# A transformer layer in float32 on one core: where the low parts of 16 weight tiles of the down projection are made

## The reference, cut to what matters

```python
h = rms_norm(x, ffn_norm_w[layer])
gate, up = jnp.split(h @ w_gate_up[layer], 2, axis=-1)
x = x + (jax.nn.silu(gate) * up) @ w_down[layer]      # (256 x 5632) @ (5632 x 2048)
```

## Time and profile before

| | us |
|---|---|
| median of 2 runs | 1143.29 (1143.13 to 1143.45) |
| the profiled execution | 1144.9 |
| its span, first to last instruction | 1142.8 |
| lies around the span | 2.1 |

### The profile page before, as it was taken

The page is one execution under the profiler, slowest core; times in us unless marked ns, Lnnn a source line. Parts: engine busy times, 40 slices in busy tenths (PEclk is TensorE's granted clock), DMA queues, the critical chain, the costliest instruction groups (busy, mean ns, idle before and its releaser), DMA issues.

```text
span 1142.8 us, 15659 instructions
## 1 busy us (share of the span) xinstructions
PE 1129.1 (99%) x5325; PEld 949.7 (83%) x5325; DVE 821.1 (72%) x1177; ACT 605.6 (53%) x856; POOL 11.6 (1%) x63
## 2 busy tenths in 40 slices
PE   7999999999999999999999999999999999999998
PEld 7988888888888888888888888888888888878887
DVE  5588787587876575667668567567577598887777
ACT  6566766668654465344344344344344455545553
POOL 3000000000000000000000000000000000000000
PEclk9999999999999999999999999999999999999999
DMA  8666454555644456666666666666666646655564
GB/s 263 192 191 204 141 173 133 160 159 159 219 161 161 166 170 183 200 193 193 191 195 193 193 193 191 194 192 186 200 192 187 208 153 215 220 197 182 195 201 166
DMA packets 102260, 213.23 MB, mean 187 GB/s; under 512 B 7065, under 2 KB 18114, under 8 KB 101954
## 3 DMA queue, kind: packets, MB, share of 16 engines
q1 hardware_dynamic: 101346, 209.30, 59.1%
q0 software_dynamic: 560, 3.15, 0.8%
q10 hardware_dynamic: 304, 0.14, 0.0%
HBM read 210.46 MB, written 2.10 MB: 186 GB/s over the span
## 4 chain that ended last, share of the span: by engine, by line
PE 89%; DVE 6%; ACT 2%; DMA 1%; issue 1%; ACTq 0%; DVEq 0%; SPq 0%
PE main L1487 45%; PE main L1490 22%; PE side L1713 7%; PE side L1716 3%; DVE w_lo L957 1%; PE side L1611 1%; PE main L1693 1%; PE main L1691 1%; PE main L1692 1%; PE side L1691 1%; PE side L1692 1%; PE side L1693 1%; DVE w_lo L1351 1%; PE side L1510 1%; DMA raw<-in_w_in 1%
## 5 line engine op out<-in xcount | busy, mean ns | idle before, releaser
L957 DVE TENSOR_TENSOR w_lo<-raw,w_hi 128x1024 fp32r<-128x1024 f32 (+3 forms) x316 | 374.9, 1191 | 249.4 <-ACT w_hi L660 245.9
L660 ACT CAST w_hi<-raw 128x1024 fp32r<-128x1024 f32 (+3 forms) x316 | 322.6, 1025 | 390.5 <-PE main L1487 384.3
L1487 PE MATMUL main<-w_hi,hT_hi 128*128 128x512 f32 (+2 forms) x1088 | 422.4, 389 | 2.4 <-DVE hT_lo L978 1.8
L1490 PE MATMUL main<-w_hi,hT_lo 128*128 128x512 f32 (+2 forms) x1088 | 418.0, 385 | 0.0
L1487 PE MATMUL main<-w_lo,hT_hi 128*128 128x512 f32 (+2 forms) x1088 | 285.5, 384 | 0.0
L1487 PEld LDWEIGHTS main<-w_hi,hT_hi 128*128 128x128 f32 x1088 | 204.9, 188 | 41.0 <-DVE hT_lo L978 3.0
L1490 PEld LDWEIGHTS main<-w_hi,hT_lo 128*128 128x128 f32 x1088 | 205.0, 188 | 37.8
L1487 PEld LDWEIGHTS main<-w_lo,hT_hi 128*128 128x128 f32 x1088 | 203.0, 188 | 39.0
L909 ACT CAST w_hi<-raw 128x1024 fp32r<-128x1024 f32 (+1 forms) x85 | 82.5, 972 | 49.8 <-PE side L1713 19.0
L1351 DVE TENSOR_TENSOR w_lo<-raw,w_hi 128x1024 fp32r<-128x1024 f32 (+1 forms) x85 | 93.1, 1120 | 5.4 <-ACT w_hi L909 5.0
L1713 PE MATMUL side<-w_hi,aT_hi 128*128 128x512 f32 x212 | 82.6, 390 | 0.1
(11 more groups left out here) (241 smaller groups left out, 968.4 us busy)
## 6 DMA issues: line engine op xcount, KB each, us to landing
raw<-in_w_gate_up SPq DMA_DIRECT2D x176, 512.0 KB, 4.4
raw<-in_w_down SPq DMA_DIRECT2D x88, 512.0 KB, 4.5
raw<-in_w_in SPq DMA_DIRECT2D x64, 512.0 KB, 3.9
raw<-in_w_out SPq DMA_DIRECT2D x32, 512.0 KB, 3.7
raw<-in_w_in SPq DMA_DIRECT2D x15, 384.0 KB, 4.3
raw<-in_w_ukv SPq DMA_DIRECT2D x8, 512.0 KB, 3.9
raw<-in_w_uq SPq DMA_DIRECT2D x8, 384.0 KB, 3.4
raw<-in_w_in SPq DMA_DIRECT2D x8, 320.0 KB, 3.1
```

Of the source, the lines that this page charges most:

```text
L660: copy(w_hi[:, slot, 0:n], raw[:, slot, 0:n]).then_inc(s_hi, 1)
L957: tt(w_lo[:, slot, 0:n], raw[:, slot, 0:n], w_hi[:, slot, 0:n].bitcast(F32), ALU.subtract)\
L1487: m = matmul(banks[t][:, 0:cols], hi[:, at[n], tok], rhs, start=(part == "hi" and k == k_first), stop=(part == "lo" and k == last))
L1490: matmul(banks[t][:, 0:cols], lo[:, at[n], tok], rhs, start=False, stop=False)
```

## The change

Of the two S items behind most Q items the first becomes an L, also a plain k tile: 8 in each of e = 0 and e = 1, 16 of the 56 plain items. For an L, DVE does nothing. ACT makes w_hi as before, waits for its own result, and writes minus w_hi into the w_lo slot (`nc.scalar.mul` by -1). Then GpSimd, which waits for that, issues a DMA from raw to w_lo that adds what it carries to what is there: w_lo = -w_hi + raw. PE starts the 8 high matmuls of an L as soon as w_hi is there, and waits for the landing of the adding DMA (s_addlo) before its 4 low ones. SP loads again into the raw slot of an L only after that landing. `lo_count` takes the L granules out of the counts of s_lo.

```diff
-    shapes = ["S" * 11 + "QSS" * 8 + "S", "S" * 3 + "QSSQSSSS" * 4 + "S"]
+    shapes = ["S" * 11 + "QLS" * 8 + "S", "S" * 3 + "QLSQLSSS" * 4 + "S"]
...
+ADDED = [x[4] for x in DOWN_ITEMS if x[0] == "L"]
...
+def lo_count(n):
+
+    return n + 1 - sum(g <= n for g in ADDED)
...
                     sp.wait_ge(s_hi, converted)
-                    sp.wait_ge(s_lo, converted)
+                    sp.wait_ge(s_lo, lo_count(converted - 1))
+                    if converted - 1 in ADDED:
+                        sp.wait_ge(s_addlo, 16 * (ADDED.index(converted - 1) + 1))
...
+            for kind, _, _, load, n, _ in DOWN_ITEMS:
+                if kind == "L":
+                    pool.wait_ge(s_neg, ADDED.index(n) + 1)
+                    pool.dma_start(w_lo[:, n % RING, :], raw[:, load % RING, :], accum_op=ALU.add).then_inc(s_addlo, 16)
...
                         hi(n, raw[:, load % RING, :], WIDE)
+                        if kind == "L":
+                            act.wait_ge(s_hi, n + 1)
+                            nc.scalar.mul(w_lo[:, n % RING, :], w_hi[:, n % RING, :].bitcast(F32), -1.0)\
+                                .then_inc(s_neg, 1)
...
-                pe.wait_ge(s_lo, n + 1)
+                if n in ADDED:
+                    pe.wait_ge(s_hi, n + 1)
+                else:
+                    pe.wait_ge(s_lo, lo_count(n))
                 for part in ("hi", "lo"):
+                    if part == "lo" and n in ADDED:
+                        pe.wait_ge(s_addlo, 16 * (ADDED.index(n) + 1))
```

More of the change, by code:

```diff
@@ L122, in down_items @@
         for kind in shape:
-            if kind == "S":
+            if kind != "Q":
                 items.append((kind, e, next(plain), load, granule, product))
@@ L159, in released @@
     for kind, _, _, first, n, q in DOWN_ITEMS:
-        if kind == "S" and load == first:
+        if kind != "Q" and load == first:
             return n + 1, 0
@@ L483, in hybrid_layer @@
         s_sum = sem("s_sum")
+        s_neg = sem("s_neg")
+        s_addlo = sem("s_addlo")
         s_corner = sem("s_corner")
@@ L1360, in paired @@
                 dve.wait_ge(s_raw[(load + 1) % RING], 16 * loads(load + 1))
-                dve.wait_ge(s_lo, n - 2)
+                dve.wait_ge(s_lo, lo_count(n - 3))
                 tt(first_two.rearrange("p (n c) -> p n c", n=2), corners,
@@ L1454, in _ @@
                         lo(n, raw[:, load % RING, :], WIDE)
-                    else:
+                    elif kind == "Q":
                         paired(load, n, q)
@@ L1746, in paired @@
                 pe.wait_ge(s_slo, p // 2 + 1)
-                pe.wait_ge(s_lo, n + 1)
+                pe.wait_ge(s_lo, lo_count(n))
                 three(m1_bank[:, :], *tokens_of(k1, 0), *weights_of(n, 0, NB), first, last).then_inc(s_used, 1)
-                pe.wait_ge(s_lo, n + 2)
+                pe.wait_ge(s_lo, lo_count(n + 1))
                 three(plain_bank[0][0][:, :], *tokens_of(k2, 0), *weights_of(n + 1, 0, NB), False, False)
@@ L1752, in paired @@
                     .then_inc(s_used, 1)
-                pe.wait_ge(s_lo, n + 3)
+                pe.wait_ge(s_lo, lo_count(n + 2))
                 three(m5_bank[:, :], *sums_of(p, 0), *weights_of(n + 2, 0, NB), first, last)
                 three(m7_bank[:, :], *sums_of(p, 2), *weights_of(n + 2, NB, WIDE), first, last).then_inc(s_used, 1)
-                pe.wait_ge(s_lo, n + 4)
+                pe.wait_ge(s_lo, lo_count(n + 3))
                 three(m6_bank[:, :], *sums_of(p, 1), *weights_of(n + 3, 0, NB), first, last)
```

## The result

The changed kernel takes 1180.2 us (1179.3 to 1181.1, 2 runs) against 1143.3: slower by 3.2%, ratio 1.0316 (1.03 to 1.0333). The forecast was 1213 in a range of 1163 to 1286. The sign and the mechanism's place are right; the stall is half as large as forecast. The profiled execution takes 1179.3 us, its span is 1177.5.

A forecast was written before the change was run, and what follows sets the result against it. PE, busy 99%, was taken to bound the kernel. 16 stalls of 3.2 us plus 1.2 us of low clock each, minus 1 us gained, gave 69.4 us more, so about 1213 us, in a range of 1163 to 1286.

The forecast's parts named there:

- D: Time of the adding DMA from POOL's issue to landing: 4.5 us for 512 KB plus 1.8 for reading the destination, 6.3.
- What bounds the kernel: PE, busy 99% of the span, sets the time; an edit gains only where PE waits.
- The slack of 3.06 us: From POOL's DMA issue at 960.70 to PE's low part at 963.76; a longer transfer makes PE wait.
- the rival of a hidden transfer: In each L the DMA lands within about 3.1 us, so PE never waits for it: 1141 us, chance 0.06.
- The rival in which the add costs no extra pass: In each L, D of 4.5 to 5 us, stall 1.4 to 1.9, clock falling behind one in three: chance 0.12.
- The DMA engines are idle where the transfer comes: From 959.7 to 962.25 their share is 0.08 against 0.64 on average, so D starts from 4.5 us.
- Three of four stalls are followed by the low clock: Behind PE's stalls of 3.2 us in L, 1.6 us lost at half clock, 1.2 us each on average.
- A clock that stays at full: Behind PE's stalls in the profile after, a sign that would make the forecast wrong.
- SP and the raw ring, cost at nothing: SP's reload of L's raw slot waits for the adding DMA but just fits: nothing, 8 us at worst.
- One us gained between e = 0 and e = 1: At the change of e, one low part less lets DVE's late additions to X shorten PE's idle: 1 us.

The follow-up runs named there:

- the kernel without the transfer: The changed kernel without the adding DMA and SP's wait on it; PE's low matmuls wait for ACT's negative copy: 1143.7 us, ratio 1.000.
- the kernel with the copy: The changed kernel with the GpSimd DMA copying raw onto the low slot in place of adding it, same waits: 1153.3 us, ratio 1.0086.
- PE alone waits: The changed kernel with the adding DMA between unread token_sums stretches; PE's low matmuls of an L wait for it, SP does not: 1215.2 us.
- SP alone waiting: The changed kernel with the adding DMA between unread token_sums stretches; SP waits for it, PE only for the negative copy: 1176.5 us.
- the kernel with both high parts first: The changed kernel with PE taking the high parts of L and the next S, then the two low parts: 1176.1 us, ratio 1.028.
- 8 L and both high parts first: The changed kernel with L behind every second Q only, and PE taking both high parts before the low parts: 1152.6 us, ratio 1.0083.

## Why the prediction was right or wrong

The mechanism forecast, a stall of PE in each L while the adding DMA is under way, is what happened. Two terms of the sum were too large, D and the clock, and one put at nothing, SP's wait, was not free. Term by term:

- *What bounds the kernel; DVE's relief is worth nothing where PE is not waiting for it.* Right, and shown by the kernel without the transfer: ratio 1.000.
- *The slack of 3.06 us.* Right: cast, negation and issue have the forecast sizes but for POOL's issue, 0.28 us in place of 0.1. The slack is 2.9 us (the low part was due at 981.41 + 0.23, the issue came at 978.71), and 4.5 - 2.9 = 1.6 us is the steady stall.
- *D = 4.5 + 1.8 = 6.3 us.* Here the size was off. The added pass was right: 1.6 us between copy and add. The base was not: I took it from POOL's loads out of HBM, and a copy between SBUF tiles lands in 2.9 us. The formula of the Trainium skill ("DMA: Bandwidth & Descriptors", section on the anatomy of one DMA on the GpSimd path), an estimate of 3.2 us for 512 KB, was thus near for the copy; the rival of a hidden transfer, beside which it stood, fell by the add's 1.6 us, for the kernel with the copy loses only 10 us.
- *The rival in which the add costs no extra pass, chance 0.12.* Its numbers came true, but for the clock, and mine did not: D of 4.5 to 5, stalls of 1.4 to 1.9 us, 1175 to 1182 us (from the median and with the 1 us gained its own terms give 1173 to 1181), against a D of 4.5 and 1180.2 us measured and my 1196 to 1240. Its reason is refuted by the copy: the pass is there, on a base that is 1.6 us lower. That the two errors cancel in D is luck.
- *The DMA engines are idle where the transfer comes*. A misreading. That window ends 1.5 us after the issue at 960.7, and a transfer of 4.5 us or more lies mostly in the next one, in which the kernel before has the engines full with SP's loads, a share of 0.98, as the row below this list shows. In the changed kernel they stay quiet only because SP is held; with SP free the transfer takes 5.8 us.
- *Three of four stalls are followed by the low clock.* Wrong here: one of 16. A clock that stays at full was named as a sign of being wrong, and behind 15 stalls it did. The stalls were 1.6 to 2.2 us, not 3.2; at that length the clock had stayed up once and fallen once before, and here it fell behind the first, of 2.2 us, and not behind the 15 others. Where a run made longer stalls the clock did fall: behind 13 of 16, most of 2.4 to 3.1 us (PE alone waits), and behind all 16 of 3.9 us. But the length of the idle time alone doesn't decide it: counted like the stalls, it stayed up behind gaps of 2.7 us (the kernel without the transfer) and 2.9 us (the one with the copy), and behind three stalls of 2.9 to 3.0 us of PE alone. What else does, the runs leave open.
- *SP and the raw ring, cost at nothing.* The fit that I worked out, 4.7 us for the load against 4.8 of room, is what the trace shows: in the chain of waits above, the cycle up to 983 goes through PE's use of the item before Q, and the next begins with the load, 4.93 us from 983.28. The two loops are equally long, 11.9 us from stall to stall here and 11.7 with SP alone waiting. What I missed is that this wait would cost nearly the whole loss by itself, 33 us. It stands beside PE's wait and is hidden by it: mending PE's side alone, as the kernel with both high parts first did, gained 4 us. I also gave the three loads behind it more room; issued together with it, they land after up to 7.2 us, which is the likely reason why my later sums fell short too.
- *One us gained between e = 0 and e = 1.* Wrong: 1.0 us lost, since the held loads make DVE later there. Even with no transfer the gap was 0.7 us longer than before and not shorter: one low part less did not bring DVE forward, because ACT's extra instruction sets it back.

The window behind that of the earlier trace rows, in the kernel before:

```profile
962.25:964.80 2.55, 2.55 (x13) 2.12 (x12) 2.55 (x4) 1.01 (x1) 0.00 (x0) 1.00 0.98 241
```

With 1.6 to 2.2 us in place of 3.2, and one dip in place of twelve, the sum of the prediction becomes 28.5 + 1.6 + 1.0 = 31 us, against 34.4 in the profiled execution. That 1215.2 us was measured with PE alone waiting, near the forecast of 1213, is no merit of the sum for the kernel asked about. There stalls and clock have about the size that I gave them, but D is long because of the loads beside it, which was not my reason.

None of the kernels is faster than the one before. The best of those with an adding transfer in use has 8 L and both high parts first, 1152.6 us. With PE at 99%, relief of another engine had nothing to give.

## What to carry to other kernels

Before work is moved off an engine, look whether the engine that sets the time ever waits for it; here it did so for 0.2 us in 82. If a transfer takes the place of an instruction, it also holds what it reads: follow every buffer to its next filling, and add up that loop with its loads, apart from the consumer's wait. Two such loops of equal length hide each other, so a mend of one gains little (4 of 37 us here), and switching each wait off alone (on tiles that nobody reads) is what tells them apart. A wait in a queue that works in order also holds everything behind it, and what was held is then issued in a burst that lands late. And when the load of the DMA engines is read from a window, the window has to cover the whole transfer.

## What the runs showed of the hardware

- A GpSimd DMA of 512 KB between SBUF tiles lands in 2.9 us as a copy, in 4.5 as an add; 256 KB as an add in 3.3; 512 KB added from HBM beside the weight loads in 7.1.
- The same add takes 5.8 to 5.9 us when SP's loads go on beside it, 4.5 when they are held.
- Four loads of 512 KB issued within 1.8 us land after 4.9 to 7.2 us; issued over 5.2 us, after 4.4 to 4.9.
- Idle times of PE of 1.6 to 2.1 us behind 15 L left the clock at 2.4 GHz, the one of 2.2 us was followed by 1.2 GHz, and so was the 1.84 us of the earlier trace rows (2.0 counted like the stalls), while gaps of 2.7 and 2.9 us, and three stalls of 2.9 to 3.0, were not: up to 3 us it goes either way. Behind all 16 stalls of 3.9 us it fell, and the loss by the clock (an estimate of 40 us) was two thirds of that of the stalls (63 us).
